# Two of four down products of every odd pair moved from the up half to the gate half of a ConvFFN pair

## What is computed

```python
def conv_ffn(h, prev, w_up, conv_w, conv_b, w_down):     # D_MODEL 1024, D_FF 2816
    T = h.shape[1]
    u = h @ w_up                                          # 1024 -> 2 * 2816 (gate | up)
    up = jnp.concatenate([prev.astype(u.dtype), u], axis=1)
    conv = conv_b + up[:, 0:T] * conv_w[0]
    for k in range(1, CONV_W):                            # CONV_W 3
        conv = conv + up[:, k:k + T] * conv_w[k]
    y = (jax.nn.silu(conv[..., :D_FF]) * conv[..., D_FF:]) @ w_down
    return y, up[:, -CONV_BUF:]
```

## Time and profile before

| | |
|---|---|
| median of 3 runs | 2560.39 us (2560.01 to 2561.55) |
| profiled execution, its own time | 2553.81 us |
| its span in the profile | 2551.5 us |
| mean granted TensorE clock | 0.988 |
| PE busy | 2411.2 us, 94% of the span |
| DVE, ACT, POOL busy | 66%, 48%, 13% |
| first 512-column half (pairs 0 to 21) | 849.9 to 1227.3 us |
| second 512-column half (pairs 44 to 65) | 1673.2 to 2091.4 us |

### The profile page before, as it was taken

How to read it: one execution, slowest core, us unless ns; L and a number is a source line. 1 busy time by engine, 2 the same in 40 slices (tenths; PEclk the granted TensorE clock), 3 DMA queues, 4 the chain that set the end, 5 groups by cost and what they waited for, 6 DMA issues and landing times.

```text
span 2551.5 us, 40501 instructions
## 1 busy us (share of the span) xinstructions
PE 2411.2 (94%) x15148; PEld 2054.7 (81%) x15148; DVE 1675.5 (66%) x2953; ACT 1218.1 (48%) x2726; POOL 334.9 (13%) x365
## 2 busy tenths in 40 slices
PE   7989999998988999999999999999989999999996
PEld 5967676665668777777899999987767779999996
DVE  4656666665235578665687768767866777766666
ACT  4444444443234645433556455554545555444443
POOL 0000000000004230000131113023122202100003
PEclk9999999999999999999999999999999999999998
DMA  7022323226542122222322222233222222232221
GB/s 271 13 93 92 114 104 115 97 105 218 200 144 82 66 87 96 91 91 91 108 79 80 75 69 82 75 115 97 90 67 91 84 91 83 83 116 83 83 83 69
DMA packets 71714, 253.50 MB, mean 99 GB/s; under 512 B 7874, under 2 KB 15426, under 8 KB 64610
## 3 DMA queue, kind: packets, MB, share of 16 engines
q1 hardware_dynamic: 71090, 250.78, 29.0%
q10 hardware_dynamic: 432, 0.15, 0.0%
HBM read 243.83 MB, written 7.07 MB: 98 GB/s over the span
## 4 chain that ended last, share of the span: by engine, by line
PE 53%; DVE 11%; ACT 3%; issue 2%; POOL 2%; DMA 0%; POOLq 0%; DVEq 0%; ACTq 0%
PE psum L2740 10%; PE psum L2741 10%; PE psum L2742 10%; PE psum L2704 6%; PE psum L2706 6%; PE psum L2705 6%; DVE t_w_lo L2508 4%; DVE t_conv L2527 3%; ACT t_w_hi L2380 2%; POOL t_stat L2102 2%; DVE t_conv L2539 1%; PE psum L2178 1%; PE psum L2682 1%; PE psum L2683 1%; PE psum L2684 1%
## 5 line engine op out<-in xcount | busy, mean ns | idle before, releaser
L2740 PE MATMUL psum<-t_h,t_w_hi 128*128 128x288 f32 (+1 forms) x2112 | 700.2, 332 | 13.5 <-DVE t_w_lo L2508 13.5
L2741 PE MATMUL psum<-t_h,t_w_hi 128*128 128x288 f32 (+1 forms) x2112 | 692.8, 328 | 0.0
L2742 PE MATMUL psum<-t_h,t_w_lo 128*128 128x288 f32 (+1 forms) x2112 | 692.0, 328 | 0.0
L2740 PEld LDWEIGHTS psum<-t_h,t_w_hi 128*128 128x128 f32 x2112 | 397.4, 188 | 57.4 <-DVE t_w_lo L2508 27.0
L2380 ACT ACTIVATE t_w_hi<-t_raw 128x1024 fp32r<-128x1024 f32 x280 | 299.2, 1069 | 266.9 <-PE psum L2706 260.0
L2560 DVE TENSOR_TENSOR t_y<-psum,t_y 128x288 f32<-128x288 f32 (+1 forms) x480 | 255.2, 532 | 257.2 <-PE psum L2706 255.7
L2741 PEld LDWEIGHTS psum<-t_h,t_w_hi 128*128 128x128 f32 x2112 | 397.3, 188 | 30.2
L2742 PEld LDWEIGHTS psum<-t_h,t_w_lo 128*128 128x128 f32 x2112 | 397.5, 188 | 28.0
L2508 DVE TENSOR_TENSOR t_w_lo<-t_raw,t_w_hi 128x1024 fp32r<-128x1024 f32 x280 | 346.0, 1236 | 87.2 <-ACT t_w_hi L2380 87.1
L2527 DVE SCALAR_TENSOR_TENSOR t_conv<-t_u,t_taps,t_conv 128x512 f32<-128x512 f32 (+2 forms) x440 | 307.2, 698 | 134.0 <-ACT t_conv L2418 129.1
L2704 PE MATMUL psum<-t_g_hi,t_w_hi 128*128 128x288 f32 (+1 forms) x1056 | 347.7, 329 | 11.6 <-DVE t_w_lo L2508 5.7
(11 more groups left out here) (215 smaller groups left out, 3361.8 us busy)
## 6 DMA issues: line engine op xcount, KB each, us to landing
t_raw<-in_ffn_w SPq DMA_DIRECT2D x264, 512.0 KB, 3.5
late_w<-in_ada_late SPq DMA_DIRECT2D x40, 1024.0 KB, 4.8
cache<-in_cache SPq DMA_DIRECT2D x64, 320.0 KB, 4.9
t_raw<-in_wo SPq DMA_DIRECT2D x16, 512.0 KB, 3.4
ada_w<-in_ada_w SPq DMA_DIRECT2D x6, 1024.0 KB, 9.0
proj_raw<-in_proj_w SPq DMA_DIRECT2D x8, 448.0 KB, 8.4
x<-in_pair_w SPq DMA_DIRECT2D x4, 768.0 KB, 5.3
x<-in_x SPq DMA_DIRECT2D x1, 2304.0 KB, 11.8
```

The costliest lines, as they stand in the source:

```text
L2740: pe.matmul(bank, t.w_hi[s][:, o], hi, start=kt == 0, stop=False)
L2741: pe.matmul(bank, t.w_hi[s][:, o], lo, start=False, stop=False)
L2742: last = pe.matmul(bank, t.w_lo[s][:, o], hi, start=False, stop=kt == KT - 1)
```

## The change

`DOWN_AT[0][0]`, the places of four down products in the 512-column half, becomes a choice by the parity of the pair. Even pairs keep 9, 11, 13, 15. Odd pairs take 3, 6, 10, 14: two products inside G, two inside U. It bears on 20 pairs: 3, 5, ... 21 and 47, 49, ... 65. Nothing else changes.

```diff
-DOWN_AT = (((9, 11, 13, 15), (4, 5, 6, 7, 10, 11, 13, 14)), ((11, 16, 21, 26), (8, 11, 14, 17, 20, 23, 26, 29)))
+DOWN_AT = ((((9, 11, 13, 15), (3, 6, 10, 14)), (4, 5, 6, 7, 10, 11, 13, 14)), ((11, 16, 21, 26), (8, 11, 14, 17, 20, 23, 26, 29)))
...
                 slots, downs = SLOT_AT[half], downs_of(n - 2)
                 places = DOWN_AT[half][len(downs) > 4]
+                if not half and len(downs) == 4:
+                    places = places[n % 2]
                 pe.wait_ge(t.lo_ready, number[s, n] + 1)
```

## The result

| | before | changed |
|---|---|---|
| median, 16 runs each | 2558.50 us | 2566.05 us |
| lowest to highest | 2553.3 to 2561.6 | 2561.2 to 2569.4 |
| ratio | | 1.0029, 95% interval 1.0022 to 1.0035 |
| profiled execution, its span | 2551.5 us | 2564.4 us |
| mean granted clock of the profile | 0.988 | 0.981 |

The change makes the kernel 0.3% slower: 7.4 us by the ratio. The forecast was +2.5 us, with a range from 2556 to 2571 us. The interval lies above the 0.2% (5.1 us) under which the prediction called two times the same: by its own bound this is slower, to which it gave 0.23, and not the same, to which it gave 0.68.

The account below looks back on a forecast made before the run. PE, busy 94% of the span, was taken to bound the kernel, so its waits and list length matter. Terms -12.1 + 17.8 - 4.5 + 1.3 = +2.5 us on 2560.4 gave 2562.9 us, range 2556 to 2571.

Parts of the forecast that it names:

- even pairs behind an odd one: 17 even pairs lose PE's wait before U for the up weights, 0.63 us each, 10.7 us in all.
- pairs 22 and 66: First pairs of the 576-column halves, behind pairs 21 and 65: down products wait less, 0.69 us each, 1.4 together.
- new wait of plain odd pairs: PE waits 1.77 us at the third down product for DVE's first addition, plus 0.11 for the slow step behind.
- pairs 5, 61, 57: Odd pairs with four norm sums between G and U: sums fill part of the new wait; -1.0, -1.0, -1.4 us.
- pair 55: Pooling products cover its waits: -1.4 us, less 0.3 for a later evacuation by ACT.
- pairs 53 and 54 together: Longer wait for DVE in 53, +2.0 us; together 0.4 faster unless the clock falls; taken as +1.3, between 0.4 and 2.2.
- Rival 3: Even pairs don't gain because their chain hangs on the old U; 2573.6 us, up to 2586; chance 0.07.
- Rival 1: No new wait at the third product in odd pairs, waits before U gone; about 2535 us; chance 0.03.
- Rival 4: First down product waits 0.3 us for its weights at step 3 in 20 odd pairs; +6, 2569 us; chance 0.06.
- Rival 5: Terms err together to the fast side: third wait 1.5, pairs 53 and 54 at no loss; 2556 us; chance 0.07.
- fifteen odd pairs are of this kind: Fifteen odd pairs, 3, 49 and 59 included, each 1.25 us longer from the new wait: +18.8, taken as +17.8.
- Rival 2: Clock falls at the new waits in all fifteen odd pairs, 1.6 us each; 2587 us; chance 0.05.

Follow-up runs that it names:

- last14_odd: Odd pairs' down products at 9, 11, 13, 14 instead of the changed kernel's 3, 6, 10, 14; 2543.4 us, 0.9947 of the kernel before.
- last15: Changed kernel with the odd pairs' last down product put back from 14 to 15; 2579.6 us, 1.0090 of the kernel before.
- add_first: Changed kernel with DVE adding the first down product ahead of G's convolution in odd pairs; 2532.1 us, 0.9901 of the kernel before.
- best: Changed kernel with odd pairs at 3, 6, 13, 14 and even pairs at 9, 11, 13, 14; 2533.1 us, 0.9901 of the kernel before.
- Third9: Changed kernel with the odd pairs' third down product at 9 instead of 10; 2590.4 us, 1.0135 of the kernel before.
- third13: Changed kernel with the odd pairs' third down product at 13 instead of 10; 2531.9 us, 0.9895 of the kernel before.
- one_in_gate: Changed kernel with odd pairs at 5, 10, 13, 14, one product in G instead of two; 2534.8 us, 0.9905 of the kernel before.

## Why the prediction was right, and which term was too small

The measured 2566.05 us lies inside the range and on the side of the forecast, but the 7.4 us are three times the 2.5 that were forecast, and more than the 5.1 up to which the prediction spoke of no change. Step by step, by the profile of the changed kernel (lengths before and after):

| term | predicted | measured |
|---|---|---|
| even pairs behind an odd one | 17 x -0.63 | -0.63 in plain pairs, -0.69 in 48, 50, 52, 56 |
| pairs 22 and 66 | -0.69 each | -0.69, -0.70 |
| new wait of plain odd pairs | 1.77 + 0.11 | 1.79 + 0.08 |
| plain odd pairs | +1.25 | +1.24 to +1.26; 7 and 63 +1.36 |
| pairs 5, 61, 57 | -1.0, -1.0, -1.4 | -0.96, -0.99, -1.42 |
| pair 55 | -1.1 | -0.96 |
| pairs 53 and 54 together | +1.3 | +1.1 |
| pairs 3 and 49 | +0.75, +1.25 | +2.73, +3.38 |
| pair 59 | +0.75 | +1.15 |

**Even pairs.** Right in mechanism and size: last14_odd and last15 show that it hangs on the last down product alone. Rival 3, the old U taking over the chain, didn't occur: in pair 10, begun at 1029.37, ACT comes to the old U at 0.53 (0.54 was predicted) and is not idle before it.

```profile
1029.90 0.58 ACT L2409 ACTIVATE t_u<-psum 128x512 f32<-128x512 f32 x1
```

**Odd pairs.** Right: the place, the releaser and the 1.8 us of the wait were forecast, and add_first shows the cause. Rival 1 would have needed the addition earlier, and that is just what add_first does, with rival 1's result: it is the change without its loss. Rival 4 (weights late at step 3) didn't occur: the first down product starts at 2.75 or 2.76 with no wait in 19 of the 20 odd pairs, and waits 0.35 in pair 53. Rival 5 didn't either: no term came out well below its forecast. The lower bound of the new wait, 1.49, can't be had from the rows named (without the 0.20 and the 0.14 it is 1.43); nothing hangs on it.

**The step that was mis-sized** is "fifteen odd pairs are of this kind": pairs 3, 49 and 59 aren't. DVE's convolution of G takes longer in them (1.95 us in pair 3, 2.09 in pair 49, against 1.54 in pair 9), as POOL is at work beside it. The timeline of DVE and POOL in pair 3 of the changed kernel:

```profile
913.60 1.95 DVE L2527 SCALAR_TENSOR_TENSOR t_conv<-t_u,t_taps,t_conv 128x512 f32<-128x512 f32 x2 [0.71 <-ACT t_conv L2418]
915.46 0.68 DVE L2558 COPY t_y<-psum 128x512 f32<-128x512 f32 x1
```

```profile
912.53 1.68 POOL L2107 TENSOR_TENSOR x<-x,t_y 128x288 f32<-128x288 f32 x2 [1.06 <-DVE t_y L1991]
```

In the run best POOL has ended before the same convolution of pair 3 begins (908.80 + 1.67 = 910.47), and the convolution takes 1.54:

```profile
910.54 1.54 DVE L2527 SCALAR_TENSOR_TENSOR t_conv<-t_u,t_taps,t_conv 128x512 f32<-128x512 f32 x2 [1.39 <-ACT t_conv L2418]
```

```profile
908.80 1.67 POOL L2107 TENSOR_TENSOR x<-x,t_y 128x288 f32<-128x288 f32 x2 [1.06 <-DVE t_y L1991]
```

So does the rest: in all twelve profiles each of the 1546 halves of such a convolution that have no POOL instruction beside them, in pairs 2 to 21 and 46 to 65, takes 0.74 to 0.76 us.

The slower convolution makes the waits of the three pairs 2.20, 2.34 and 2.20 instead of 1.79: 1.4 us in all. Second, in pairs 3 and 49 the clock falls behind this wait, 1.5 us each. Together that is 4.4 us, against the 4.1 (6.6 less 2.5) by which the pairs' sum exceeds the forecast; small terms of the other sign make up the rest.

**Rival 2, the clock,** was given one chance in twenty as a thing of all fifteen pairs, at 1.8 us. In that form it didn't occur: in three profiles with this wait (the change twice, last15) 36 plain odd pairs waited 1.79 to 1.92 us and the clock fell in none. But it had a second form that I didn't price outside pair 53: a few pairs whose wait is a little longer. It also set two measures side by side: the 1.65 and 2.37 of the earlier trace rows are idle times of the profile, 1.77 is from start to start. As idle time the new wait is 1.62, next to the 1.65, and in pairs 3, 49 and 59 it is 2.03, 2.17 and 2.03, between the two rows. The rule of the Trainium skill that was weighed there (TensorE: Matmul & The Clock Gate, section A second HAM failure mode: psum-queue depth-cycling) speaks of idle times that come often. Third9, whose only difference is 0.69 us more to wait for the same bank, does swing between the two levels in 13 of 16 odd pairs, which agrees with it; at 1.8 us the same wait, as often, brought no swing. That the bank is no condition is seen in pair 46, where the clock fell in 8 of 12 profiles behind a wait for POOL.

**Pairs 53 and 54** came out as a whole, +4.5 and -3.4, and that is in part luck. The prediction counted one fall of the clock in pair 53, 3.4 us long; it lasted 6.8 us there (clock 0.85 over the pair). And it overlooked that in the kernel before the clock had fallen in pair 54, behind the wait of the earlier trace rows:

```profile
1856.19:1882.82 26.63, 22.66 (x89) 17.39 (x88) 17.82 (x22) 8.21 (x15) 9.46 (x8) 0.94 0.19 60
```

After the change it stayed at 1.00, though the wait was still 2.51 us. Pair 54 lasts 24.24 without a fall (third13) and 25.90 with one (one_in_gate), so the fall that went is worth some 1.7 us; that the one in pair 53 lasted longer costs about 1.0 (22.22 in last15, where it lasted 3.4 us, against 23.20). The rest of the -3.4 is time that pair 54 no longer waits.

## What to carry to other kernels

When a product is moved forward on one engine, look up where its consumer stands in the other engine's list: a buffer is given back not when its data are ready, but when that list comes to it, and here the fix is to move the addition into the idle time ahead of a waiting instruction (1.0029 to 0.9901). When a chain starts from the end of one operation (here the last down product, whose single weight buffer starts the next pair's splits), a step's worth of other work placed behind that operation is free cover: one product moved by one step is worth 0.5 to 1%. And price a new wait at the longest of its instances too, not only at the typical one: of the change's waits for the addition, those of pairs 3, 49 and 53 are three of the four longest, and the clock fell behind these alone; in pairs 3 and 49 that took 1.5 us each, where the longer wait itself added 0.4 and 0.55.

## What the runs showed of the hardware

- At the third product, a PE wait of 1.8 to 1.9 us never brought the granted clock down (36 instances in three profiles); one of 2.2 to 2.35 us did in 7 of 9 (pairs 3, 49 and 59 of the same three profiles); one of 2.4 us and above did in 13 of 16 (third9). A fall costs some 1.5 us here: about 8 matmuls at 0.43 us instead of 0.23.
- The length of the wait alone doesn't decide it. Behind the idle time of 2.37 us in pair 46 the clock fell in 8 of the twelve profiles (in three of them for 6.8 us instead of 3.4), behind that of 2.48 to 2.57 us in pair 54 in 7; in pair 57 of last14_odd it fell with no idle time longer than 1.43 us, which the kernel before has there without a fall. What tips it isn't shown.
- A convolution on DVE (two instructions of 128x512) took 1.54 us alone and 1.95 to 2.09 with POOL at work beside it (pairs 3, 59 and 49 of the change).
- Two executions of the same stretch ahead of the change differ by 6.3 us with the clock at 0.97 and 0.98, as much as the change itself does. One profile against another can't tell 0.3%; the lengths of plain pairs, which repeat within some 0.03 us, can.
- From the start of the first matmul behind a group to ACT's start on the group's bank it is 0.19 to 0.20 us, from the end of DVE's addition to PE's start on the freed bank 0.15, and the second matmul after a wait comes 0.08 to 0.11 us later than in a running row.
